# Merging the three attention branches of a head pair on GpSimd instead of VectorE

## The reference, cut to what matters

```python
o_cmp, o_sel, o_win, win_new = nsa_fn(q, _rope(q, pos), rows, win_rows, pos)
gate = jax.nn.sigmoid(pr['nsa_gate'].astype(jnp.float32)).reshape(B, T, 3, NSA_HEADS, 1)
no = gate[:, :, 0] * o_cmp + gate[:, :, 1] * o_sel + gate[:, :, 2] * o_win
no = no.reshape(B, T, NSA_WIDTH) * jax.nn.silu(pr['nsa_g'].astype(jnp.float32))
go, gdn_new, conv_new = _gated_delta(...)
mix = jnp.concatenate([ro, no, go], axis=-1).astype(x.dtype)
y = x + _rmsnorm(mix @ lp['w_out'], lp['norm_post'])
```

## Time and profile before

| | |
|---|---|
| runs | 2449.62, 2452.12, 2456.47 us; median 2452.12 |
| profiled execution: span from first to last instruction | 2458.1 us |
| profiled execution: time beside the span | none is given |
| busy over the span | PE 2156.3 us (88%), PEld 1601.7, DVE 1261.5 (51%), ACT 788.6, POOL 418.2 |
| joint stage of the first layer | 369.0 to 687.8 us |
| joint stage of the second layer | 1582.0 to 1905.3 us |
| granted TensorE clock, mean of the span | 0.900 of full speed |

### The profile page before, as it was taken

One profiled execution on the slowest core, in us unless ns is written; L12 is line 12 of the kernel. 1 busy time (PEld: TensorE's weight loads), 2 busy tenths in 40 slices (PEclk: granted clock), 3 DMA queues, 4 the chain that ended last, 5 costly groups with the idle time before them and its releaser, 6 DMA issues. The chain is left out here.

```text
span 2458.1 us, 36105 instructions
## 1 busy us (share of the span) xinstructions
PE 2156.3 (88%) x12280; PEld 1601.7 (65%) x12280; DVE 1261.5 (51%) x2982; ACT 788.6 (32%) x1678; POOL 418.2 (17%) x648
## 2 busy tenths in 40 slices
PE   6999868978879999997889997688888899999977
PEld 3644456767758888885345444577776788888853
DVE  2244365666536666654223533656674466666532
ACT  2211113334434544440212211134243444444302
POOL 0110001001143333410001100011111433443100
PEclk9999868889889999997989997698797799999869
DMA  5452100000086867753045521000001877788331
GB/s 184 156 196 69 43 22 14 1 10 1 10 200 150 182 156 174 186 113 116 2 152 169 180 68 38 23 1 1 9 1 36 193 168 155 175 187 180 78 116 39
DMA packets 173056, 243.10 MB, mean 99 GB/s; under 512 B 50714, under 2 KB 132282, under 8 KB 172192
## 3 DMA queue, kind: packets, MB, share of 16 engines
q1 hardware_dynamic: 143328, 147.27, 23.3%
q0 software_dynamic: 29536, 93.43, 14.6%
HBM read 223.69 MB, written 25.50 MB: 101 GB/s over the span
## 5 line engine op out<-in xcount | busy, mean ns | idle before, releaser
L609 PE MATMUL bank<-W,hT 128*128 128x512 f32 (+3 forms) x1152 | 446.8, 539 | 17.2 <-DMA W<-in_w_in 12.9
L609 PEld LDWEIGHTS bank<-W,hT 128*128 128x128 f32 x1152 | 216.3, 194 | 205.9 <-issue 172.2
L978 PE MATMUL bank<-XT,W 128*128 128x256 f32 (+1 forms) x768 | 250.8, 462 | 0.0
L1035 POOL DMA_DIRECT2D SHARED<-in_cache_nsa_kv x256 | 152.0, 594 | 455.5 <-DVE RP L948 352.2
L1218 POOL TENSOR_TENSOR work<-UP,SHARED 128x512 f32<-128x512 f32 x56 | 72.2, 1293 | 829.4 <-DVE UP L1503 505.5
L1233 ACT ACTIVATE Pr<-bank,mx 128x31 f32<-128x31 f32 (+4 forms) x192 | 85.6, 446 | 335.8 <-DVE mx L1428 321.2
L967 ACT ACTIVATE XT<-bank 128x512 f32<-128x512 f32 x256 | 140.0, 593 | 137.6 <-PE bank L960 137.6
L1035 POOL DMA_DIRECT2D PS<-in_cache_nsa_kv x256 | 150.5, 588 | 138.7 <-issue 126.4
L978 PEld LDWEIGHTS bank<-XT,W 128*128 128x128 f32 x768 | 134.9, 190 | 49.7 <-issue 36.9
L960 PE MATMUL bank<-CF,RP 128*128 128x128 f32 x1024 | 147.5, 290 | 12.8 <-DVE RP L948 11.4
L372 DVE COPY UP<-bank 128x512 f32<-128x512 f32 (+3 forms) x36 | 21.5, 605 | 235.1 <-PE bank L609 234.9
(11 more groups left out here) (396 smaller groups left out, 3668.9 us busy)
## 6 DMA issues: line engine op xcount, KB each, us to landing
SHARED<-in_cache_nsa_kv SPq DMA_DIRECT2D x256, 128.0 KB, 5.5
SHARED<-in_cache_nsa_kv POOLq DMA_DIRECT2D x256, 128.0 KB, 5.1
PS<-in_cache_nsa_kv SPq DMA_DIRECT2D x256, 128.0 KB, 5.9
PS<-in_cache_nsa_kv POOLq DMA_DIRECT2D x256, 128.0 KB, 5.6
W<-in_w_in SPq DMA_DIRECT2D x48, 512.0 KB, 3.7
XS<-scratch_conv_p POOLq DMA_DIRECT2D x24, 384.0 KB, 4.4
PW<-in_state_nsa_win SPq DMA_DIRECT2D x16, 512.0 KB, 3.9
Wo<-in_w_out SPq DMA_DIRECT2D x4, 2048.0 KB, 11.8
```

What stands on the lines that cost most here:

```text
L609: return nc.tensor.matmul(bk((c * NTILE + t) % BANKS)[:, 0:b - a], hT[:, k, t * P:(t + 1) * P], W[:, k // 2, k % 2, 0:b - a], start=(k == ...
L978: mm = nc_(self.v).tensor.matmul(out, self.v['W1'][:, kv, s, :], seg[:, s], start=(s == 0), stop=(s == SEG // PAIRS - 1))
L1035: e.dma_start(where[side * HD:(side + 1) * HD, slot, :, :], A['cache_nsa_kv'][l, page].rearrange("(p r) a g d -> p r (a g d)", r=PAIRS)[:, ...
```

## The change

VectorE keeps the three steps that make the factors, into one of two buffers `fac`, and no longer waits for `merged`: it waits for the sums (`exped`) and, from the third group on, for the merge two groups back. It tells GpSimd by `scaled`. GpSimd waits for `merged` and `scaled` and does the product, two additions in place of the reduction, and the gating. Since GpSimd's merges must have a place in its list, it now walks `ORDER` too: a merge at its unit's place, and each mask behind the later of its tile's "ready2" and the turn of the step before. `first_pages` stays behind the loop.

```diff
--- before.py
+++ after.py
@@ -1116,7 +1116,7 @@
     PT = sb(scope, "PT", [P, BACK, 4, P])
     mx = sb(scope, "mx", [P, DEEP, 2])
     SUM = sb(scope, "SUM", [P, 2, 2, 3])
-    fac = sb(scope, "fac", [P, 2, 3])
+    fac = sb(scope, "fac", [P, 2, 2, 3])
     OB = sb(scope, "OB", [P, 2, 3, HD])
     NO = sb(scope, "NO", [P, 2, HD])
     bk, cf, cb, ident, MIX = v['bk'], v['cf'], v['cb'], v['ident'], v['MIX']
@@ -1180,8 +1180,14 @@
             dn += [f"ss{hp}{q}{j}" for j in "nms"] + (["vm1"] if what == "add01" else [])
         ends[what, t] = dn[-1]
 
-    with stage(["dve_s", "act_s", "pe_s", "loaded", "gl", "outs", "kv", "score", "shift", "exped", "turned", "copied", "used", "link_s", "merged", "freed", "masked"]) as \
-            (block, (dve_s, act_s, pe_s, loaded, gl, outs, kv, score, shift, exped, turned, copied, used, link_s, merged, freed, masked)):
+    mask_after = {}
+    for t, k in steps:
+        i = steps.index((t, k))
+        at = [ORDER.index(("ready2", t))] + ([ORDER.index(("turn", steps[i - 1]))] if i else [])
+        mask_after[ORDER[max(at)]] = (t, k)
+
+    with stage(["dve_s", "act_s", "pe_s", "loaded", "gl", "outs", "kv", "score", "shift", "exped", "turned", "copied", "used", "link_s", "merged", "freed", "masked", "scaled", "pool_s"]) as \
+            (block, (dve_s, act_s, pe_s, loaded, gl, outs, kv, score, shift, exped, turned, copied, used, link_s, merged, freed, masked, scaled, pool_s)):
         dve, act, pe = Steps(dve_s, dn), Steps(act_s, an), Steps(pe_s, pn)
         pool = Steps(masked, [f"nn{t}.{k}" for t, k in steps])
 
@@ -1209,14 +1215,39 @@
 
         @block.gpsimd
         def _(e):
-            for i, (t, k) in enumerate(steps):
-                n = ROWS[t]
+            links = [0]
+
+            def link(ins):
+                links[0] += 1
+                ins.then_inc(pool_s, 1)
+                e.wait_ge(pool_s, links[0])
+
+            def mask(t, k):
+                n, i = ROWS[t], steps.index((t, k))
                 dve.wait(e, f"nt1{t}")
                 if i >= 2:
                     t2, k2 = steps[i - 2]
                     dve.wait(e, f"tt{t2}.{k2}")
                 pool.done(e, f"nn{t}.{k}", nc.gpsimd.tensor_tensor(NTs(t, k)[0:n, :, 0:n], NTt_[t][0:n, :, 0:n],
                                                                    b_(cf('level', P)[0:n, k, 0:n], 1, [n, H4, n]), ALU.mult))
+
+            def merge(k):
+                qt, br, h = units[GROUP * (k + 1) - 1]
+                first = h - 1
+                e.wait_ge(merged, k + 1)
+                e.wait_ge(scaled, k + 1)
+                link(nc.gpsimd.tensor_tensor(OB[:, :, :, :], OB[:, :, :, :], b_(fac[:, k % 2, :, :], 3, [P, 2, 3, HD]), ALU.mult))
+                link(nc.gpsimd.tensor_tensor(NO[:, :, :], OB[:, :, 0, :], OB[:, :, 1, :], ALU.add))
+                nc.gpsimd.tensor_tensor(NO[:, :, :], NO[:, :, :], OB[:, :, 2, :], ALU.add).then_inc(freed, 1)
+                e.wait_ge(freed, k + 1)
+                link(nc.gpsimd.tensor_tensor(MIX[:, qt, 256 + first * HD:256 + (first + 2) * HD], NO[:, :, :].rearrange("p h d -> p (h d)"),
+                                             U[qt][:, NG + first * HD:NG + (first + 2) * HD], ALU.mult))
+
+            for what, x in ORDER:
+                if (what, x) in mask_after:
+                    mask(*mask_after[what, x])
+                if what == "unit" and x >= BACK and (x - BACK) % GROUP == GROUP - 1:
+                    merge((x - BACK) // GROUP)
             dve.wait(e, "n33")
             first_pages(e, A, l, v, 1)
 
@@ -1430,15 +1461,12 @@
                     qt, br, h = units[u - BACK]
                     first, k = h - 1, (u - BACK) // GROUP
                     gates = U[qt][:, NGATE:NGATE + 3 * NH].rearrange("p (b h) -> p h b", b=3)[:, first:first + 2, :]
-                    e.wait_ge(merged, k + 1)
-                    link(nc.vector.tensor_scalar(fac[:, :, :], SUM[:, k % 2, :, :], 1e-30, None, ALU.max))
-                    link(nc.vector.reciprocal(fac[:, :, :], fac[:, :, :]))
-                    link(nc.vector.tensor_tensor(fac[:, :, :], fac[:, :, :], gates, ALU.mult))
-                    link(nc.vector.tensor_tensor(OB[:, :, :, :], OB[:, :, :, :], b_(fac[:, :, :], 3, [P, 2, 3, HD]), ALU.mult))
-                    nc.vector.tensor_reduce(NO[:, :, :], OB[:, :, :, :].rearrange("p h b d -> p h d b"), AX.X, ALU.add).then_inc(freed, 1)
-                    e.wait_ge(freed, k + 1)
-                    link(nc.vector.tensor_tensor(MIX[:, qt, 256 + first * HD:256 + (first + 2) * HD], NO[:, :, :].rearrange("p h d -> p (h d)"),
-                                                 U[qt][:, NG + first * HD:NG + (first + 2) * HD], ALU.mult))
+                    e.wait_ge(exped, GROUP * (k + 1))
+                    if k >= 2:
+                        e.wait_ge(freed, k - 1)
+                    link(nc.vector.tensor_scalar(fac[:, k % 2, :, :], SUM[:, k % 2, :, :], 1e-30, None, ALU.max))
+                    link(nc.vector.reciprocal(fac[:, k % 2, :, :], fac[:, k % 2, :, :]))
+                    nc.vector.tensor_tensor(fac[:, k % 2, :, :], fac[:, k % 2, :, :], gates, ALU.mult).then_inc(scaled, 1)
 
             def sampled_states(q, hp):
                 if hp == 0:
```

## The result

The changed kernel took 2418.14 us (median of 4 runs, 2412.14 to 2436.73), the kernel before 2451.14 us beside it: ratio 0.9867, interval 0.9826 to 0.9909. Ten later runs of the same kernel gave 2427.9 us against 2454.41 us, ratio 0.9883 (0.9848 to 0.9918), so some 27 to 33 us. The profiled execution's span is 2410.6 us (that run took 2412.14), so it is one of the kernel's quicker ones; the profiled execution of before lies above its median.

A forecast was written before the change was run, and what follows sets the result against it. TensorE, the fullest engine, was taken to bound the joint stages by its waits; waits -17.5, clock -8, lock +1.5 and end +22 gave -2 us off the median 2452.12, so 2450 us, range 2428 to 2466 us.

The forecast's parts named there:

- The waits: TensorE's thirty waits through a merge in both joint stages: of 34.0 us, 17.5 us would close.
- all 34 us shut: Rival for the joint stages: every TensorE wait through a merge closes, 34 us, giving 2434 us; chance 0.36.
- The clock: TensorE's granted clock in the joint stages: shorter waits spare some time at 0.50, 8 us gained.
- the share: Part of the 24.5 us at stake in the joint stages' low clock that was taken as gained: a third.
- the forecast's own price of 0.36: Cost in the joint stage of each us at the lower clock: 0.36 us, from 6.1 us for some 17.
- its eight stretches: Stretches at clock 0.50 in the joint stages that begin at one of the thirty waits, 68 us together.
- The end: End of each joint stage: page loads now behind GpSimd's last merge, 11 us a layer, 22 us lost in two.
- The lock: GpSimd and VectorE sharing a port pair at the merges: three holds of 0.5 us, 1.5 us lost.
- the lock's rival of 16 us: Each merge holds one VectorE instruction before a TensorE wait by 0.5 us: 16 us lost, 2464.5 us; chance 0.18.
- more of the waiting goes: Rival for the joint stages: all 34.0 us of waits shut, 2434 us, or 2417 without the eight stretches; chance 0.36.
- a clock above 0.87: Sign in the changed kernel's profile: granted clock of the first layer's joint stage above 0.87.
- wrong if the last copy OB comes over 20 us a layer earlier: Condition at the joint stage's end: the forecast is wrong if its last copy OB comes over 20 us a layer earlier.

The follow-up runs named there:

- a_again: The changed kernel run again with no edit and a second profile; 2427.9 us, ratio to the kernel before 0.9883.
- twice: The changed kernel with GpSimd's first addition of each merge made three times, same sum; 2431.4 us, ratio to the kernel before 0.9898.
- b_again: The kernel before run again with no edit and a second profile; 2455.86 us, ratio to the kernel before 0.9985.
- the delay runs: The changed kernel with two, four or five scratch reductions on VectorE behind the factors of every merge; 2430.2, 2443.4 and 2468.1 us.
- pages_early: The changed kernel with GpSimd's issue of the first pages moved ahead of its last merges; 2404.72 us, ratio to the kernel before 0.9819.
- delay_4: The changed kernel with four scratch reductions on VectorE behind the factors of every merge; 2443.4 us, ratio to the kernel before 0.9959.
- delay_5: The changed kernel with five scratch reductions on VectorE behind the factors of every merge; 2468.1 us, ratio to the kernel before 1.0050.

## Why the prediction was wrong

By its steps, with means over two profiles (four layers) of each kernel where they differ: body 318.3 and 294.1 us, idle 45.6 and 37.8, busy 272.2 and 255.8, at 0.50 87.6 and 52.3, tail 4.2 and 14.2.

- **The waits: right.** 17.5 us forecast; idle time fell by 17.6 us in the first pair of profiles and by 15.6 by the means (2 x 7.8). The working that kept TensorE's times and moved VectorE's starts was good to 2 us, and "all 34 us shut" was wrong.
- **The clock: the step that failed.** "Because the waits shrink and don't vanish, and the two thirds of TensorE's idle time that no merge causes stay, I take a third: 8 us gained." That waits bring the clock down was right; the term was four times too small. The low clock fell by 35 us a layer, 71 in two, and TensorE's busy time by 32.6 us (2 x 16.3), 0.46 us for each, inside the prices found with the program unchanged (0.43 by a_again, 0.45 by `twice`, 0.49 between the layers of b_again). Of the 25 us that were missing, the share (all instead of a third) is worth 17 at the forecast's own price of 0.36, and the price the rest. The price is in part a matter of counting: 0.36 was taken from the length of a stretch, while TensorE's busy time in the same fell by 7.3 us, 0.43 for each; and a straight line through all runs of one kernel gives 0.32 us of the whole time (before) and 0.37 (changed) for each us at 0.50. So the share is the error.
- **What the share overlooked.** The forecast let each stretch at 0.50 stay or go, in proportion to the waits. The 71 us are close to the 68 of its eight stretches by chance, for few stretches went and the others became shorter: without the first 25 us of each body, four layers of before have 35 stretches of 265 us together, four of the changed kernel 28 of 130. And by the delay runs the sum goes in a step: a hold that is shorter by 0.6 us has spared most of it. Why a stretch becomes shorter no run here shows.
- **The end: right.** 22 us forecast, 20.0 measured (2 x 10.0), and pages_early shows that it is the pages. A merge took 2.43 us instead of 2.9 (product 0.83 for 0.99, hand-offs 0.08 for 0.15); the first page load came 16.7 us after the last step of the delta rule ended (641.49 + 0.42 to 658.56), "some 15" forecast; the drain took 3.4 us, "about 3" forecast.
- **The lock: right to leave small.** Two-input VectorE steps still doubled at times, but most kept their length: all VectorE steps that both kernels have took 3.9 us more together in the two bodies of the first pair, on the path or not. The eight steps L1476 (L1448 of the earlier trace rows) have a lower median than before, 682 instead of 1108 ns, below; the lock's rival of 16 us, at 0.18, is out, and `twice` says so with more such work.

Line L1476 of the changed kernel, ns min, median and max:

```profile
L1476 DVE TENSOR_TENSOR SS<-SS,SLp x8: 681/682/1525, 493.1 to 1709.9; 128x512 f32<-128x512 f32 x8
```

The sum by the means is -15.6 - 32.6 + 20 = -28 us; the two comparisons gave -33 and -27. It leaves out the rest of the program, which took 1802 and 1803 us in the changed kernel's profiles and 1816 and 1809 in those of before; over all thirteen profiles it takes 1796 to 1816, so no effect of the change on it is shown. The rival "more of the waiting goes" named 2417 us with all eight stretches gone, and the result is 2418, but not by its way, so that hit is luck: the waiting closed no further than forecast, only the clock did. The sign "a clock above 0.87" and the condition "wrong if the last copy OB comes over 20 us a layer earlier" both came true. Some 5 us of the first comparison's 33 are chance, by the second one and the means.

## What to carry to other kernels

Where TensorE's granted clock falls behind waits, don't scale the low clock with the waiting. Here the last 0.6 us of the 2.9 us of hold decided over most of what the change spared; keep none and all as bounds, and let a run with a delay put back say where between them it lies. When a step moves to another engine, look at what that engine's list holds behind it: here eight page issues cost 20 us until they were put ahead of the last merges. And where short waits remain on the fullest engine, cheap spare matmuls in them can pay for themselves through the clock; place them by the trace, wait by wait.

## What was not expected of the hardware

- The same program has different stretches at 0.50 from execution to execution, and even from layer to layer: 40.8 and 60.4 us in the first layer of two profiles of the changed kernel, 40.5 and 67.5 us in the two layers of `twice`. With 0.45 us for each that is a spread of about 12 us a layer. The runs of the changed kernel (2409.93 to 2444.15 us) have 405 to 498 us at 0.50 by their granted clocks, and their times follow it (correlation 0.92 over 14 runs).
- The low clock changed by 35 us a layer in the profiles, 25 by all runs, for 0.6 us of hold more (delay_4 to delay_5), while the idle time changed by 2.8.
- GpSimd's additions of 128x128 took 0.45 us and its 128x384 product 0.83, with hand-offs of 0.07 to 0.08 us between them; VectorE's product of the same shape took 0.56.
